# A two-block network kernel on one core: six places of hand-written order changed

## Time and profile before

| | |
|---|---|
| runs (us) | 1084.61, 1084.67, 1086.76; median 1084.67 |
| the profiled execution | 1088.07, its span 1086.3 |
| TensorE (PE) busy | 1062.1 us, 98% of the span |
| weight loads (PEld) | 915.8 us, 84% |
| VectorE (DVE) | 789.6 us, 73% |
| ScalarE (ACT) | 611.6 us, 56% |
| GpSimd (POOL) | 221.4 us, 20% |
| read from HBM | 179.44 MB, 168 GB/s over the span |
| granted TensorE clock | 0.999 on the mean |

### The profile page before, as it was taken

How to read it: one execution, slowest core, us unless ns; L and a number is a source line. 1 busy time by engine, 2 the same in 40 slices (tenths; PEclk the granted TensorE clock), 3 DMA queues, 4 the chain that set the end, 5 groups by cost and what they waited for, 6 DMA issues and landing times.

```text
span 1086.3 us, 18718 instructions
## 1 busy us (share of the span) xinstructions
PE 1062.1 (98%) x7143; PEld 915.8 (84%) x7143; DVE 789.6 (73%) x1092; ACT 611.6 (56%) x965; POOL 221.4 (20%) x234
## 2 busy tenths in 40 slices
PE   7999999999999999999999999999999999999997
PEld 6997798888888888789888888998777889888886
DVE  7997867878885668778888666688868775566543
ACT  6766376656664576855666454644654455544532
POOL 0125483122220021001222201551100001211200
PEclk9999999999999999999999999999999999999999
DMA  8553172656667476354666574555561654666552
GB/s 247 171 176 119 40 237 76 175 158 191 193 193 266 145 149 175 117 142 132 193 193 180 198 284 122 194 187 184 160 172 45 227 158 129 183 179 189 193 194 78
DMA packets 219748, 183.12 MB, mean 169 GB/s; under 512 B 43265, under 2 KB 197614, under 8 KB 219678
## 3 DMA queue, kind: packets, MB, share of 16 engines
q1 hardware_dynamic: 215710, 171.43, 52.7%
q0 software_dynamic: 3392, 8.66, 2.5%
q10 hardware_dynamic: 576, 2.07, 0.5%
HBM read 179.44 MB, written 2.69 MB: 168 GB/s over the span
## 4 chain that ended last, share of the span: by engine, by line
PE 79%; DVE 12%; DMA 3%; issue 2%; ACT 2%; POOL 1%; SPq 1%; DVEq 0%; POOLq 0%; ACTq 0%
PE bank L288 21%; PE bank L282 13%; PE bank L284 12%; PE bank L283 12%; PE bank L289 10%; DVE ring L417 3%; PE bank L295 2%; PE bank L1252 1%; DVE arena L1710 1%; DVE arena L1805 1%; DVE stat L1803 1%; DMA arena<-in_kv_w_up 1%; PE bank L375 1%; PE bank L2182 1%; SPq L3416 1%
## 5 line engine op out<-in xcount | busy, mean ns | idle before, releaser
L417 DVE TENSOR_TENSOR ring<-ring,arena 128x2048 fp32r<-128x2048 f32 (+1 forms) x138 | 310.3, 2252 | 114.0 <-ACT arena L411 112.4
L282 PE MATMUL bank<-arena 128*128 128x512 f32 (+3 forms) x980 | 343.9, 351 | 2.3 <-DVE ring L417 1.5
L288 PE MATMUL bank<-arena 128*128 128x512 f32 x960 | 335.7, 396 | 0.0
L411 ACT ACTIVATE arena<-ring 128x2048 fp32r<-128x2048 f32 (+1 forms) x145 | 272.3, 1880 | 96.9 <-DMA ring<-in_ffn_w_out 43.3
L289 PE MATMUL bank<-arena,ring 128*128 128x256 f32 x960 | 267.2, 278 | 0.0
L284 PE MATMUL bank<-arena 128*128 128x512 f32 (+3 forms) x720 | 264.8, 368 | 0.0
L283 PE MATMUL bank<-ring,arena 128*128 128x512 f32 (+2 forms) x560 | 216.1, 386 | 0.0
L288 PEld LDWEIGHTS bank<-arena 128*128 128x128 f32 x960 | 180.1, 188 | 42.6
L282 PEld LDWEIGHTS bank<-arena 128*128 128x128 f32 x980 | 185.4, 189 | 27.7 <-issue 4.3
L289 PEld LDWEIGHTS bank<-arena,ring 128*128 128x128 f32 x960 | 180.6, 188 | 0.0
L284 PEld LDWEIGHTS bank<-arena 128*128 128x128 f32 x720 | 135.6, 188 | 22.2
(11 more groups left out here) (338 smaller groups left out, 1271.8 us busy)
## 6 DMA issues: line engine op xcount, KB each, us to landing
ring<-in_ffn_w_in SPq DMA_DIRECT2D x80, 512.0 KB, 5.1
ring<-in_ffn_w_out SPq DMA_DIRECT2D x44, 512.0 KB, 4.5
ring<-in_w_gate_up SPq DMA_DIRECT2D x40, 512.0 KB, 5.0
ring<-in_w_in SPq DMA_DIRECT2D x18, 1024.0 KB, 5.0
ring<-in_a_w_rkv SPq DMA_DIRECT2D x12, 1024.0 KB, 5.7
ring<-in_w_down SPq DMA_DIRECT2D x22, 512.0 KB, 3.7
ring<-in_a_w_o SPq DMA_DIRECT2D x4, 1024.0 KB, 7.9
arena<-in_ffn_w_in SPq DMA_DIRECT2D x8, 512.0 KB, 5.0
```

The costliest lines, as they stand in the source:

```text
L282: nc.tensor.matmul(dst, stationary[0], moving[0], start=start, stop=False)
L288: nc.tensor.matmul(dst[:, :], stationary[0], both_parts, start=start, stop=False)
L411: nc.scalar.activation(buf(hi_of(n), 0, w, arena12), ring[:, r, 0:w], ACT.Copy).then_inc(hi_ready, 1)
L417: on.tensor_tensor(ring12[:, r, 0:w], ring[:, r, 0:w], buf(hi_of(n), 0, w, arena12).bitcast(F32), ALU.subtract).then_inc(split_ready, 1)
```

## The change

It changes order in six places and takes out the fillers named above.

1. The second `bonus_sums` goes from inside the value product to between the banks of head pairs (before bank 4), into PSUM bank 0 instead of 6, without its filler; ACT copies it after the values.
2. SP issues the late inverse blocks of both token tiles each ahead of a slot of `w_o` instead of behind it.
3. At the feed-forward fronts TensorE turns x of tile 1 ahead of the first `early_turn`, and the four `keep_busy` calls (8 matmuls) go. In front 0 the low part of early weights 0 moves back into the layer before it, ahead of the last `o_lo`, and that of early weights 1 moves ahead of `turn_dve`.
4. `squares(1, 1)` goes ahead of `kv_weights_hi(1)`.
5. TensorE takes attention heads 4 to 15 singly: turn, scores, values. ACT and DVE follow that order, the rotary adds are given out one head at a time, and the halves of the `o_w` split move.
6. The state-space norm: the add and the gate of tile 0 come ahead of the half split, the add of tile 1 ahead of the scaling of tile 0, the gate of tile 1 behind the attention gate of tile 0, and the turned low part of tile 0 ahead of the scaling of tile 1.

```diff
@@ ffn_front_dve
             if f != 1:
-                early_lo(dve, f, 0 if f == 0 else 1)
+                early_lo(dve, f, 1)
             turn_dve(dve, turn, 0, 4, hi, lo)
-            if f == 0:
-                early_lo(dve, f, 1)
@@ ffn_pe
             early(1, 0)
+            xn_turns(pe, i - 1, 1)
             early_turn(0, 0)
-            xn_turns(pe, i - 1, 1)
             early_turn(1, 0)
-            keep_busy(pe, 4, 2)
             early(0, 1)
@@ rwkv_pe
-                    if a == 1 and c == 4:
-                        keep_busy(pe, 1, 7)
-                    mm = by_columns(bank[6][:, a * H + 2 * c:a * H + 2 * c + 2],
+                    mm = by_columns(bank[(6, 0)[a]][:, a * H + 2 * c:a * H + 2 * c + 2],
...
-                if s == 2:
-                    pe.wait_ge(tok_evac, 4)
-                    bonus_sums(1)
-
-            pe.wait_ge(bonus_copied, NT)
+
+            pe.wait_ge(bonus_copied, 1)
             pe.wait_ge(tok_evac, 4)
             for l in range(PAIR_BANKS):
+                if l == 4:
+                    pe.wait_ge(v_evac, 1)
+                    bonus_sums(1)
...
+            pe.wait_ge(bonus_copied, NT)
             pe.wait_ge(v_evac, 4)
             key_values(0)
@@ rwkv_act
-            act.wait_ge(bonus_summed, 2)
-            nc.scalar.activation(bon[:, H:2 * H], bank[6][:, H:2 * H], ACT.Copy).then_inc(bonus_copied, 1)
             act.wait_ge(tok_mm, 5)
...
+            act.wait_ge(bonus_summed, 2)
+            nc.scalar.activation(bon[:, H:2 * H], bank[0][:, H:2 * H], ACT.Copy).then_inc(bonus_copied, 1)
@@ rwkv_dve
             o_lo(1, 0)
+            early_lo(dve, 0, 0)
             o_lo(1, 1)
@@ mla_pe
             scores(3)
-            values(0)
             q_rope(3)
             turn_p(2)
+            values(0)
             swapped(2)
...
-            for h in range(4, H, 2):
-                for x in range(2):
-                    turn_p(h + x)
-                    if h + 2 < H:
-                        scores(h + 2 + x)
-                for x in range(2):
-                    values(h - 2 + x)
-                if h == 4:
+            for h in range(4, H):
+                turn_p(h)
+                if h + 2 < H:
+                    scores(h + 2)
+                if h == 6:
                     swapped(3)
-                if h == 12:
+                values(h - 2)
+                if h == 13:
                     o_turns(0)
@@ mla_act
             latents_hi(1, 0)
+            squares(1, 1)
             kv_weights_hi(1)
-            squares(1, 1)
...
-            for h in range(4, H - 2, 2):
+            for h in range(4, H - 2):
                 evac(h)
-                if h == 6:
+                if h == 12:
                     split_act_half(act, o_w + 1, 1)
-                evac(h + 1)
                 exps(h + 2)
-                exps(h + 3)
@@ mla_dve
-            maxima(4)
-            maxima(5)
-            roped(2, range(0, 2))
-            maxima(6)
-            maxima(7)
-            roped(2, range(2, 4))
             split_half(dve, o_w, 1)
-            for h in range(8, H):
+            sined(2)
+            for h in range(4, 8):
                 maxima(h)
...
+                roped(h + 4)
+            maxima(8)
+            sined(3)
+            roped(12)
+            for h in range(9, 12):
+                maxima(h)
+                roped(h + 4)
@@ block_dve
             carried_on(1, 1)
-            split_half(dve, FIRST["ssd_proj"], 0)
...
+            y_gated(0, y_summed(0))
+            split_half(dve, FIRST["ssd_proj"], 0)
+            y_variance(0)
+            second_sum = y_summed(1)
             dve.wait_ge(yg_gain_landed, 16)
             y_normed(0)
             attention_gated(0)
-            y_variance(1)
+            y_gated(1, second_sum)
             split_half(dve, FIRST["ssd_proj"], 1)
             emitted[dve] = FIRST["ssd_proj"] + 1
+            y_variance(1)
+            turn_dve(dve, TURN_SSD, 0, 0, B_SQ, B_SQ_LO)
             y_normed(1)
-            turn_dve(dve, TURN_SSD, 0, 0, B_SQ, B_SQ_LO)
             attention_gated(1)
             ahead(dve, FIRST["ssd_proj"] + 1, split_dve)
@@ weights_sp
             rwkv_inverse_sp(sp)
+            rwkv_inverse_late_sp(sp, 0)
             rows_of("w_o", A["a_w_o"][0], 2, range(0, 1))
-            rwkv_inverse_late_sp(sp, 0)
+            rwkv_inverse_late_sp(sp, 1)
             rows_of("w_o", A["a_w_o"][0], 2, range(1, 2))
-            rwkv_inverse_late_sp(sp, 1)
```

More of the change, by code:

```diff
@@ L2238, in mla_pe @@
             scores(5)
-            for h in range(4, H, 2):
-                for x in range(2):
-                    turn_p(h + x)
-                    if h + 2 < H:
-                        scores(h + 2 + x)
-                for x in range(2):
-                    values(h - 2 + x)
-                if h == 4:
+            for h in range(4, H):
[3 more added lines that the diff above has]
+                if h == 6:
                     swapped(3)
-                if h == 12:
+                values(h - 2)
+                if h == 13:
                     o_turns(0)
-            for x in range(2):
-                values(H - 2 + x)
+            values(H - 2)
+            values(H - 1)
             def o_tiles(a, s):
@@ L2357, in mla_act @@
             q_even(2)
+            o_w = FIRST["o_w"]
+            split_act_half(act, o_w, 0)
             exps(1)
-            o_w = FIRST["o_w"]
             q_rotary(2)
             evac(0)
-            split_act_half(act, o_w, 0)
+            split_act_half(act, o_w, 1)
             exps(2)
@@ L2365, in mla_act @@
             evac(1)
-            split_act_half(act, o_w, 1)
+            split_act_half(act, o_w + 1, 0)
             q_rotary(3)
@@ L2369, in mla_act @@
             evac(2)
-            split_act_half(act, o_w + 1, 0)
             exps(4)
@@ L2469, in q_odd_heads, with sined, roped @@
                                         ALU.mult).then_inc(q_odd, 1)
[L2471 to L2479, removed]
+            def sined(s):
+                dve.wait_ge(perm_mm, Q_AT[f"p{s}"])
+                link(dve, nc.vector.tensor_tensor(q_sined[s % 2], bank[PERM_BANK[s]][:, T:2 * T], const("sinT"), ALU.mult))
+            def roped(h):
+                s, rows_ = h // 4, slice(h % 4 * ROPE, (h % 4 + 1) * ROPE)
+                dve.wait_ge(q_cos, s + 1)
+                nc.vector.tensor_tensor(qT[rot, h, :], q_cosed[s % 2][rows_, :], q_sined[s % 2][rows_, :],
+                                        ALU.add).then_inc(q_roped, 1)
             def maxima(h):
@@ L2508, in mla_dve @@
             q_odd_heads(1)
-            roped(0)
+            sined(0)
+            for h in range(4):
+                roped(h)
             maxima(0)
@@ L2512, in mla_dve @@
             maxima(1)
-            roped(1)
+            sined(1)
+            for h in range(4, 8):
+                roped(h)
             maxima(2)
@@ L2516, in mla_dve @@
             o_w = FIRST["o_w"]
+            split_half(dve, o_w, 0)
             maxima(3)
-            split_half(dve, o_w, 0)
-            maxima(4)
-            maxima(5)
-            roped(2, range(0, 2))
-            maxima(6)
-            maxima(7)
-            roped(2, range(2, 4))
             split_half(dve, o_w, 1)
-            for h in range(8, H):
+            sined(2)
+            for h in range(4, 8):
                 maxima(h)
-                if h == 9:
-                    roped(3, range(0, 2))
-                if h == 11:
-                    roped(3, range(2, 4))
-                if h == 13:
-                    normalized(0)
+                roped(h + 4)
[5 more added lines that the diff above has]
+                roped(h + 4)
+            maxima(12)
+            maxima(13)
+            normalized(0)
+            maxima(14)
+            maxima(15)
             split_half(dve, o_w + 1, 0)
@@ L3222, in mixed, with y_summed @@
                                             ALU.add).then_inc(mix_ready, 1)
-            for a in range(NT):
+            def y_summed(a):
                 for q in range(2):
@@ L3227, in block_dve, with y_gated @@
                     op = nc.vector.tensor_tensor(y[:, a, cells], bank[4 + 2 * a + q][:, :], toks(B_DX)[:, a, cells], ALU.add)
-                if a == 1:
-                    y_variance(0)
-                link(dve, op)
+                return step(op)
+            def y_gated(a, summed):
+                dve.wait_ge(dve_step, summed)
                 nc.vector.tensor_tensor(y[:, a, :], y[:, a, :], toks(B_Z)[:, a, :], ALU.mult).then_inc(yz_ready, 1)
```

## The result

The changed kernel takes 1096.68 us (median of 6 runs, 1095.35 to 1099.51) beside 1086.77 (6 runs, 1084.61 to 1090.17) of the kernel before: 1.0093 times, 95% interval 1.0078 to 1.0109. The forecast was 1079.5, faster. It is slower by 10 us.

The account below looks back on a forecast made before the run. TensorE, busy 1062.1 of 1086.3 us, was taken as the bound. Six places summed to -5.2 us, a span of 1081.1; with the 1.6 us between span and median carried over, 1079.5, range 1077.8 to 1082.3.

Parts of the forecast that it names:

- Place 1: Bonus sums among the pairs: TensorE comes earlier but waits for the same DVE mask; 0, with 0.2 us either way.
- The clock: Rival: without fillers the granted clock falls to 1.2 GHz in the three fronts, 5 us each, 1094 us; chance 3%.
- Place 2: Inverse blocks: late blocks issued ahead of w_o land before TensorE needs them, so its wait goes; -1.1 us.
- Place 3: Feed-forward fronts: earlier turns and scaling, no fillers; -1.6 us in front 0, -0.2 in each other, sum -2.0.
- Place 4: Squares ahead of ACT's weight copy: TensorE's wait at the turn and a later loss to DVE shrink; -1.2 us.
- Place 5: Attention heads taken singly: waits 1.6 us shorter, split bursts 0.8 longer; -0.8 us.
- Place 6: State-space norm: the wait for the attention gate goes, but the next product waits right behind it; -0.1 us.

Follow-up runs that it names:

- run 1: The kernel before with place 1 alone: 1092.12 us, 1.0036 times the kernel before.
- run 2: The changed kernel with one added wait, so that GpSimd's multiply starts only after DVE's chain: 1090.31 us, 1.0023 times the kernel before.
- run 6: The changed kernel with place 1 put back and the fronts' fillers kept in the new order: 1089.03 us, 1.0011 times the kernel before.
- run 9: The kernel before with place 3 alone: 1089.33 us, 1.0004 times the kernel before.
- run 10: The kernel before with places 4 and 5 alone: 1087.70 us, 0.9994 times the kernel before.
- run 12: The kernel before with place 2 alone: 1089.51 us, 1.0009 times the kernel before.
- run 13: Run 11's kernel with one edit, x turned ahead of the early turn: 1088.40 us, 0.9994 times the kernel before.
- run 3: The changed kernel with place 1 put back as before: 1088.34 us, 1.0002 times the kernel before.
- run 5: The kernel before with only the fillers of the three fronts taken out: 1087.52 us, 0.9998 times the kernel before.
- run 8: Kernel before with places 3 to 6, fronts' fillers kept, and w_o slots 0 and 1 ahead of the first inverse's save: 1088.86 us, 1.0011.
- run 11: Kernel before with places 4 to 6, early w_o, and of place 3 only DVE's low parts and the fillers' removal: 1084.05 us, 0.9960.
- run 14: Run 11's kernel once more, beside run 13: 1085.91 us, 0.9966 times the kernel before.
- run 4: The changed kernel with 46 fillers in the long wait ahead of bank 4: 1098.24 us, 1.0090 times the kernel before.
- run 7: The changed kernel with GpSimd's multiply waiting for DVE's chain and 9 fillers ahead of bank 4: 1088.30 us, 1.0008 times the kernel before.

## Why the prediction was wrong

**Place 1 (0, with 0.2 either way): the step that failed.** "Nothing removed on TensorE shortens that chain", true, but something lengthened it. I followed what DVE and ACT do when TensorE ends 1.5 us earlier, and left out GpSimd, whose memsets wait for the end of the same product. Its multiply moved from 126.54 to 125.33 and into the last steps of the chain: +4.4 us. Runs 1 and 2 show it. On the whole time this place, with the clock that fell behind its wait, is most of the loss: the ratio is 1.0093 as changed, 1.0023 with the multiply held back and 1.0008 with the clock kept as well. The Trainium skill, page SBUF — State Buffer, section Who interferes with whom, has this rule: VectorE and GpSimd share a pair of ports as an exclusive lock, a VectorE operation with two SBUF inputs and a GpSimd operation that reads SBUF exclude each other, and the first to start has it to its end. The trace agrees: the held step reads SBUF twice, the memsets (121.81 to 125.4) held none of the steps beside them, and the mask, which reads PSUM, ran its 1.41 us beside the multiply in the kernel before.

**The clock (3%, in the fronts).** The rival had the right mechanism at the wrong place. I let idle times of 1.8 us stand for all. With GpSimd in DVE's way the wait is 6.4 us, and the fall behind it costs 1.8; with GpSimd out of the way (run 2) it is 2.1, and the fall costs 1.5. The row of before was no safe ground either: with place 1 as before and a wait of 1.8 to 2.1 us, the clock fell in the profiled executions of runs 6, 9, 10, 12 and 13 (0.72 on the mean of 127 to 133 us) and stayed at 1.00 in those of before and of runs 3, 5, 8, 11 and 14. At this length the clock may fall or not, and a fall costs 1.4 to 1.7 us in those traces. What I cited of the Trainium skill, TensorE: Matmul & The Clock Gate, section What's actually happening, that the slow clock is the default and activity releases it, agrees with runs 4 and 7, where the clock stayed at 1.00 with fillers in the wait.

**Place 2 (-1.1): the wait went, but it was no wait of the program.** TensorE's 1.1 us at the inverses are gone as said (0.17 idle left), and they are gone in runs 1, 5, 9 and 10 too, which have the old order. I had read one execution, in which the last of the first four late blocks landed 5.2 us after its issue. I also took w_o for the reason of the save's 6.4 us. The save takes 6.9 in the changed kernel and 6.1 with w_o landed long before (run 8). What stands beside it in every trace is POOL's two gain loads, which I had passed over. So w_o came 2 us behind a save that is no quicker, and was late not by 1 us but by 4 and more (issued at 151.04, ACT idle until 158.64). Net +1.5 in the changed kernel and -0.7 in run 3, where the traces with the old order have -1.3 to -1.6.

**Place 3 (-2.0).** Front 0 -1.5 (forecast -1.6), fronts 1 and 2 -0.2 each (-0.2), and the wait in the fillers' place is 0.4 idle, as said. What no step of mine had is the pace of the feed-forward behind it, some 2.5 us at the median if it is the pace (runs 13, 14). Place 3 alone gives no measurable difference (run 9, 1.0004).

**Place 4 (-1.2)** stands in the ledger with -1.3, but kernels without it win 0.3 to 1.5 us in the same stage, so the forecast priced a wait that is shorter or missing in other executions. **Place 5 (-0.8)** measured -0.5, the same in all twelve traces that have it; the waits of the heads are gone but for 0.3, and the split bursts cost what they were priced at. **Place 6 (-0.1)**: -0.9 at the turn and +0.8 at the next product, -0.1 in sum.

**The last output slot (+1.8)** belongs to no place. Its transfer took 7.4 us instead of 4.9; of the 16 DMA engines' work a thin rest is left for the last 2.5 us, and one packet of code was fetched during the transfer, 0.8 us behind its issue. The chain of waits, and the queues in 876.5 to 884.2 (packets, MB, share):

```profile
876.71 7.40 DMA ring<-in_w_out
```

```profile
q1 hardware_dynamic: 370, 1.38, 50.1%
q8 instruction: 1, 0.02, 0.8%
```

In the 68 transfers of this product's four slots in the 17 traces, 62 took 4.7 to 5.3 us; the other six took 5.5 to 7.4, and five of them had a code packet in them, four within 1.3 us of their issue. Four more transfers had a packet 4.4 us or more behind their issue, and took 4.9 to 5.1. That the packet delays the transfer, and that fewer instructions of TensorE moved it onto this slot, is argued, not tried.

**Sum.** Hold +4.4, clock +1.8, place 2 +1.5, fronts -1.9, pace +4.1 in this execution, latents -1.3, heads -0.5, norm -0.1, slot +1.8: +9.8 of the 9.7 measured. The range was too narrow because it was made of the ends of my own terms, and the two largest losses, the held step and the pace, are not among them. The pace's 4.1 us depend on which execution was profiled: the one of before has two fast feed-forwards of three.

## What to carry to other kernels

- When an edit makes an engine finish earlier, list every engine that waits for that point, those far from the critical path too, and look at what they start and what it shares with a chain at its end. Here a single wait on GpSimd was worth some 7 us.
- A filler or a small piece of work in front of a wait may be what keeps the granted clock. Price a longer idle time with the fall, even if the present ones do no harm.
- A wait that ends with the landing of a transfer can belong to one execution alone. Before a forecast takes it as a gain, look for it in a second execution. Here two of the six terms, 2.3 of the 5.2 us, rested on such waits.
- When times of one program spread by several us, compare the spreads as well as the medians, and start-to-start distances inside long dense loops as well as waits: a change may take away a good case that only some executions have.

## What the runs showed of the hardware

- A VectorE step of 0.22 us took 4.50 to 4.57 us beside a GpSimd multiply that began 0.03 to 0.07 us earlier, in all four profiled kernels that have the new place 1 and leave the multiply where it falls.
- The same dense loop runs at two paces with a granted clock of 1.00: 231 to 233 ns or 233 to 241 ns for one matmul of 512 columns in turn with one of 256, kept for a whole feed-forward of 111 or 113 us.
- A wait of 1.8 to 2.1 us of TensorE in dense work was followed by a granted clock of 0.50 in six profiled executions (runs 2, 6, 9, 10, 12 and 13) and left it at 1.00 in six (before, runs 3, 5, 8, 11 and 14).
- Two saves of 512 KB from the same buffer landed after 2.6 us and after 5.6 to 7.5 us; the second has two loads of 512 KB by GpSimd's queue beside it.
